# Two MLP halves apart: the up half in pairs with seven products for eight, activations through DRAM, the down half in blocks of three pairs

## The reference, cut to what matters

```python
def sq_relu_mlp(u, w1, w2):
    return jnp.square(jax.nn.relu(u @ w1)) @ w2      # w1: 1024 x 4096, w2: 4096 x 1024

h = post_norm_residual(h, y, g1, ln_g[i, 0], ln_b[i, 0])
h = post_norm_residual(h, sq_relu_mlp(modulate(h, sh2, sc2), mlp_w1[i], mlp_w2[i]), g2, ln_g[i, 1], ln_b[i, 1])
```

## Time and profile before

| what | us |
|---|---|
| median of 3 runs (lowest, highest) | 3314.88 (3314.34, 3315.09) |
| profiled execution, its span from first to last instruction | 3312.7 |
| PE busy in it | 3142.2 (95%) |
| DVE, ACT, POOL busy | 2118.3, 1329.6, 960.4 |
| mean DMA rate | 71 GB/s |

### The profile page before, as it was taken

How to read it: one execution, slowest core, us unless ns; L and a number is a source line. 1 busy time by engine, 2 the same in 40 slices (tenths; PEclk the granted TensorE clock), 3 DMA queues, 4 the chain that set the end, 5 groups by cost and what they waited for, 6 DMA issues and landing times.

```text
span 3312.7 us, 36526 instructions
## 1 busy us (share of the span) xinstructions
PE 3142.2 (95%) x14623; PEld 2589.1 (78%) x14623; DVE 2118.3 (64%) x2816; ACT 1329.6 (40%) x1877; POOL 960.4 (29%) x425
## 2 busy tenths in 40 slices
PE   7999888889999999978899999998999899999997
PEld 3888777778888888767788888887887788888886
DVE  4725477676777777585766565567697655555554
ACT  4311588454333333442633333335227443333332
POOL 0001466244444443310443333313000022222220
PEclk9999999999999999989999999999999999999999
DMA  7435211212233322111011111111111111111121
GB/s 231 145 115 178 88 45 49 89 44 72 101 102 102 102 98 81 45 41 51 26 57 52 51 51 51 51 58 52 32 52 58 58 45 51 51 51 51 51 64 51
DMA packets 190482, 235.72 MB, mean 71 GB/s; under 512 B 9671, under 2 KB 149562, under 8 KB 190314
## 3 DMA queue, kind: packets, MB, share of 16 engines
q1 hardware_dynamic: 173338, 172.90, 16.8%
q10 hardware_dynamic: 8352, 30.41, 2.6%
q0 software_dynamic: 8624, 30.09, 2.4%
HBM read 217.64 MB, written 15.73 MB: 70 GB/s over the span
## 4 chain that ended last, share of the span: by engine, by line
PE 74%; DVE 13%; ACT 8%; issue 3%; DMA 1%; POOL 0%; DVEq 0%; SPq 0%; ACTq 0%; POOLq 0%
PE psum L609 24%; PE psum L610 24%; PE psum L611 24%; DVE page_r L620 2%; DVE small L1413 2%; DVE small L742 1%; DVE PT_lo L620 1%; ACT temp L923 1%; ACT page_r L615 1%; ACT prob L1379 1%; DVE U_lo L620 1%; ACT U_hi L615 1%; DMA page<-in_ada_w_dram 1%; DVE H L1525 1%; PE psum L788 1%
## 5 line engine op out<-in xcount | busy, mean ns | idle before, releaser
L609 PE MATMUL psum<-U_hi,page_r 128*128 128x512 f32 x2108 | 832.4, 395 | 23.9 <-DVE page_r L620 11.1
L610 PE MATMUL psum<-U_lo,page_r 128*128 128x512 f32 x2108 | 826.2, 392 | 0.0
L611 PE MATMUL psum<-U_hi,page_r 128*128 128x512 f32 x2108 | 826.0, 392 | 0.0
L620 DVE TENSOR_TENSOR page_r<-page,page_r 128x1024 fp32r<-128x1024 f32 (+2 forms) x239 | 344.4, 1447 | 357.8 <-ACT page_r L615 350.6
L615 ACT CAST page_r<-page 128x1024 fp32r<-128x1024 f32 (+2 forms) x323 | 337.4, 1047 | 397.6 <-DVE page L640 95.2
L609 PEld LDWEIGHTS psum<-U_hi,page_r 128*128 128x128 f32 x2108 | 399.3, 189 | 117.3 <-DVE page_r L620 16.2
L611 PEld LDWEIGHTS psum<-U_hi,page_r 128*128 128x128 f32 x2108 | 399.0, 189 | 84.2
L610 PEld LDWEIGHTS psum<-U_lo,page_r 128*128 128x128 f32 x2108 | 399.4, 189 | 81.1
L609 PE MATMUL psum<-page_r,act_page_r 128*128 128x512 f32 x1176 | 457.5, 389 | 0.0
L610 PE MATMUL psum<-page_r,act_page_r 128*128 128x512 f32 x1176 | 457.5, 389 | 0.0
L2243 ACT ACTIVATE temp<-psum 128x512 f32<-128x512 f32 x192 | 114.6, 597 | 849.9 <-PE psum L611 805.6
(11 more groups left out here) (343 smaller groups left out, 4594.7 us busy)
## 6 DMA issues: line engine op xcount, KB each, us to landing
page<-in_mlp_w_dram SPq DMA_DIRECT2D x128, 512.0 KB, 4.1
page<-in_ada_w_dram SPq DMA_DIRECT2D x48, 512.0 KB, 5.0
page<-in_w_in_dram SPq DMA_DIRECT2D x38, 512.0 KB, 4.1
page<-in_w_up_dram SPq DMA_DIRECT2D x32, 512.0 KB, 4.1
page<-in_w_down_dram SPq DMA_DIRECT2D x32, 512.0 KB, 4.1
ada_land<-in_ada_w_dram ACTq DMA_DIRECT2D x24, 512.0 KB, 4.4
sum_page<-in_ada_w_dram ACTq DMA_DIRECT2D x12, 512.0 KB, 5.5
act_page<-in_ada_w_dram ACTq DMA_DIRECT2D x12, 512.0 KB, 8.6
```

The lines of the kernel that those rows point to most:

```text
L609: pe.matmul(out, l_hi, r_hi, start=start, stop=False, skip_group_check=read_between)
L610: pe.matmul(out, l_hi, r_lo, start=False, stop=False, skip_group_check=read_between)
L611: return pe.matmul(out, l_lo, r_hi, start=False, stop=stop, skip_group_check=read_between)
L620: return dve.tensor_tensor(lo, src, hi.bitcast(F32), ALU.subtract).then_inc(*k.lo.inc(*key))
```

## The change

Each MLP is now two phases.

Up phase (`pe_up_phase`): the 32 feature groups are 16 pairs, and a pair is again a 2 x 2 matrix (feature group by width half on one side, width half by token half on the other), made by the same seven products of 12 matmuls. The operands on the token side (U and its sums T1, T2, T4) are made once per MLP, on ACT, DVE and POOL, the sums of weights for every pair (`pool_up_sums`: e, f, c, g). Results come out of three banks A, B, C by copies of ACT and sums of DVE, named 11, 12, 21, 22 (token half first). After the square, POOL makes the four sums that the down half needs (`pool_act_folds`) for 14 of the pairs, and SP stores all to DRAM. The first three pairs do their products 1 and 2 before the second half of the tokens is transposed.

Down phase (`pe_products`, 5 blocks of 2, 3, 3, 3, 3 pairs): activations come back from DRAM by SP, split on ACT and DVE; weights by quarter, gated and summed by POOL, low parts of products 1, 2, 6, 7 on DVE and 5, 4, 3 on POOL. The last two pairs are done directly by `pe_down_tile`, 8 tiles in a row. In mlp0, H lies in DRAM during the up phase (`d_h`), and its place takes the ada pieces, four in each of the pairs 3 to 14, loaded by SP.

```diff
-BLOCKS = D_FF // (P * FB)
+PAIRS = D_FF // (2 * P)
+START = 3
+SIZES = (2, 3, 3, 3, 3)
+LAST = len(SIZES)
+RAW_PAIRS = PAIRS - sum(SIZES)
+FOLDED = PAIRS - RAW_PAIRS
...
+UP_ORDER = [(n, p) for n in range(START) for p in ("1", "2")] + [(n, p) for p in REST for n in range(2)] + \
+    [(2, p) for p in REST] + [(n, p) for n in range(START, PAIRS) for p in PRODUCTS]
...
+def up_weight(n, p):
+    if n < START:
+        return {"6": "a", "7": "c", "5": "e", "4": "d", "3": "b"}[p]
+    return {"1": "a", "2": "b", "6": "f", "7": "c", "5": "e", "4": "d", "3": "g"}[p]
...
+    def product(n, p):
+        key = (name, n, p)
+        if n < START and p in ("1", "2"):
+            on.wait_ge(*k.lo.at("w", k.unit(name, n).s))
+        else:
+            on.wait_ge(*k.lo.at("up", *key))
+        if p == "1":
+            held[n, "A"] = k.banks.take(on, ("up", name, n, "A"), (k.relu_done, (name, n, "21")), slot=n % 3)
+        elif p == "2":
+            held[n, "B"] = k.banks.take(on, ("up", name, n, "B"), (k.summed, (name, n, "11")), slot=3 + next(bank) % 5)
+        elif p == "7":
+            held[n, "C"] = k.banks.take(on, ("up", name, n, "C"), (k.summed, (name, n, "12")), slot=3 + next(bank) % 5)
+        elif p == "6":
+            on.wait_ge(*k.copied.at(name, n, "1"))
+        elif p == "5":
+            on.wait_ge(*k.copied.at(name, n, "6"))
+        elif p == "4":
+            on.wait_ge(*k.copied.at(name, n, "7"))
+        else:
+            on.wait_ge(*k.summed.at(name, n, "22"))
+        b = held[n, {"2": "B", "7": "C", "4": "C"}.get(p, "A")]
+        w_hi, w_lo = up_parts(k, name, n, p)
+        u_hi, u_lo = up_operand(k, p, 0), up_operand(k, p, 1)
+        for j in range(4):
+            if n < START:
+                if p in ("1", "2"):
+                    on.wait_ge(*k.lo.at("u", before.name, 0, j + (4 if p == "2" else 0)))
+                else:
+                    on.wait_ge(*k.lo.at("t", name, p, j))
+            s = slice(j * P, (j + 1) * P)
+            m = three_passes(pe, k.psum[:, b, :], w_hi[:, s], w_lo[:, s], u_hi[:, j, :], u_lo[:, j, :],
+                             p in ("1", "2", "7") and j == 0, j == 3, read_between=True)
+        m.then_inc(*k.up_done.inc(name, n, p))
...
+        product(n, p)
+        if p == PRODUCTS[-1] and name == "mlp0" and n in ADA_SUM_BEHIND:
+            part = ADA_SUM_BEHIND.index(n)
+            pe_ada_sum(k, pe, on, 1, part, ada_acc(k, part), slot=3 + next(bank) % 5)
...
+def sp_ada(k, sp, on, u):
+    if u.n >= ADA_RING:
+        on.wait_ge(*k.ada_x_ok.at(*k.ada_late[u.n - ADA_RING].ada))
+    else:
+        on.wait_ge(*k.h_dma[u.n].at("park"))
+        on.wait_ge(*BOUNDARY[0].hat(k, u.n))
+    sp.dma_start(u.raw, u.pieces[0][1]).then_inc(*k.ada_in[u.n % ADA_RING].inc(u.n))
...
+    for n in range(START, PAIRS):
+        folds(n - 1)
+        ada(n + 1, 0)
+        raw(n + 2, 0)
+        if n == PAIRS - 1:
+            weights(0, "11")
+            acts(0, "1")
+            weights(0, "21")
+            acts(0, "2")
+            weights(0, "12")
+            weights(0, "22")
+        square("11", n)
+        square("22", n)
+        ada(n + 1, 1)
+        raw(n + 2, 1)
+        square("12", n)
+    acts(0, "6")
...
+        on.wait_ge(*k.ada_summed.at(1, 5))
+        on.wait_ge(*k.ada_summed.at(1, 4))
+        on.wait_ge(*k.ada_x_ok.at(1, 5, KT - 1))
+        for t in range(TT):
+            on.wait_ge(*k.h_dma[t].at("park"))
+            on.wait_ge(*before.hat(k, t))
+            sp.dma_start(k.H[:, t, :], k.d_h[t]).then_inc(*k.h_dma[t].inc("back"))
+    folds(PAIRS - 1)
...
+    def step(what, x, y, op):
+        pool.tensor_tensor(at(what), at(x), at(y), op).then_inc(*k.up_folded.inc(name, n, what))
+        on.wait_ge(*k.up_folded.now())
+    for e in range(2):
+        if n >= START:
+            on.wait_ge(*k.raw_in[up_raw_page(n, e)].at(name, n, e))
+        elif e:
+            on.wait_ge(*k.raw_in[up_raw_page(n, e)].at(name, n, e))
         else:
...
+            u = k.unit(name, n)
+            on.wait_ge(*k.raw_in[u.page].at(u.n))
+            on.wait_ge(*k.lo.at("w", u.s))
+    on.wait_ge(*k.down_done.at(before.down, TT - 1, 1))
+    if n == 1:
+        on.wait_ge(*k.up_done.at(name, 2, "2"))
+    elif n >= 2:
+        on.wait_ge(*k.up_done.at(name, n - 2, "5"))
+    step("e", "c", "d", ALU.add)
+    if n < START:
+        step("c", "a", "c", ALU.subtract)
+        step("a", "e", "a", ALU.subtract)
+        step("b", "b", "a", ALU.subtract)
+        return
+    on.wait_ge(*(k.up_done.at(name, 0, "3") if n == START else k.up_done.at(name, n - 1, "6")))
+    step("f", "e", "a", ALU.subtract)
+    step("c", "a", "c", ALU.subtract)
+    if n < START + 2:
+        on.wait_ge(*k.up_done.at(name, 2, "6" if n == START else "3"))
+    else:
+        on.wait_ge(*k.up_done.at(name, n - 2, "3"))
+    step("g", "b", "f", ALU.subtract)
...
+    for which in ("11", "12", "22", "21"):
+        on.wait_ge(*k.squared.at(name, n, which))
+    if n:
+        on.wait_ge(*k.store5.at(name, n - 1, "fold 5"))
+        on.wait_ge(*k.store3.at(name, n - 1, "fold 3"))
+    step("5", s1, a21, a22, ALU.add)
+    step("7", a21, a11, a21, ALU.subtract)
+    on.wait_ge(*k.store11[n % 3].at(name, n, "11"))
+    step("6", a11, s1, a11, ALU.subtract)
+    step("3", s4, a12, a11, ALU.subtract)
...
+    act_up_start(k, act, on, name, before)
+    for n in range(START, PAIRS):
+        more = n + 1 < PAIRS
+        hi(n, "7")
+        copy(n, "1")
+        hi(n, "5")
+        square(n, "11")
+        hi(n, "4")
+        copy(n, "6")
+        hi(n, "3")
+        copy(n, "7")
+        if more:
+            hi(n + 1, "1")
+            hi(n + 1, "2")
+        square(n, "22")
+        if more:
+            hi(n + 1, "6")
         else:
...
+            parts(0, "1")
+        square(n, "12")
+        if not more:
+            parts(0, "2")
+        square(n, "21")
+    squares_stored(k, on, name)
...
+    dve_up_start(k, dve, on, name, before)
+    for n in range(START, PAIRS):
+        more = n + 1 < PAIRS
+        lo(n, "7")
+        ada(n, 0)
+        lo(n, "5")
+        if name == "mlp0" and n - 1 in ADA_SUM_BEHIND:
+            dve_mod(k, dve, on, 1, ADA_SUM_BEHIND.index(n - 1))
+        total(n, "11")
+        lo(n, "4")
+        ada(n, 1)
+        lo(n, "3")
+        if more:
+            lo(n + 1, "1")
+        ada(n, 2)
+        total(n, "22")
+        if more:
+            lo(n + 1, "2")
+        else:
+            dve_down_weight(k, dve, on, name, 0, "1")
+            dve_down_act(k, dve, on, name, 0, "1")
+        total(n, "12")
+        ada(n, 3)
+        if more:
+            lo(n + 1, "6")
+    squares_stored(k, on, name)
+    for g, (b, p) in enumerate(SEQUENCE):
+        stage = (name, b)
+        if b:
+            ready = lambda tt: on.wait_ge(*k.h_added.at((name, b - 1), "3", TPC - 1))
+        elif name == "mlp0":
+            ready = lambda tt: on.wait_ge(*k.h_dma[tt].at("back"))
+        else:
+            ready = lambda tt: on.wait_ge(*before.hat(k, tt))
+        for t in range(TPC):
+            if t == 0 and g + 1 < len(SEQUENCE):
+                dve_down_act(k, dve, on, name, *SEQUENCE[g + 1])
+            dve_quarter_tile(k, dve, on, stage, p, t, 1.0 if b else alpha, ready)
+            if t == 0 and g + 1 < len(SEQUENCE):
+                dve_down_weight(k, dve, on, name, *SEQUENCE[g + 1])
+        if (b, p) == (0, "1") and name == "mlp0":
+            dve_mod(k, dve, on, 1, 5)
+        if (b, p) in LAST_GATE_AT:
+            dve_last_gate(k, dve, on, name, LAST_GATE_AT[b, p])
...
+def pool_up_start(k, pool, on, name, b):
+    raw = lambda p, j: up_raw(k, p)[:, j, :]
+    for n in range(2):
+        pool_up_sums(k, pool, on, name, n, b)
+    for p, src, ready in (("4", "6", "6"), ("7", "3", "5")):
+        for j in range(4):
+            on.wait_ge(*k.t_vector.at(name, ready, j))
+            if p == "4":
+                x, y = raw("4", j), raw("6", j)
+            else:
+                x, y = raw("3", j), raw("7", j)
+            pool.tensor_tensor(raw(p, j), x, y, ALU.subtract).then_inc(*k.t_pool.inc(name, p, j))
+    pool_up_sums(k, pool, on, name, 2, b)
+    pool_act_folds(k, pool, on, name, 0)
+    pool_up_sums(k, pool, on, name, 3, b)
+    pool_act_folds(k, pool, on, name, 1)
...
+def pool_gate(k, pool, on, name, b):
+    if not GATE[name]:
+        return
+    on.wait_ge(*k.gate_ok.at(*GATE[name]))
+    for i, quarter in enumerate(("11", "21", "12", "22")):
+        v, c = down_raw(k, b, quarter), int(quarter[1]) - 1
+        on.wait_ge(*k.down_in[b % 2][i].at(name, b))
+        gate = k.row_gate[:, c * CH:(c + 1) * CH].unsqueeze(1).to_broadcast([P, SIZES[b], CH])
+        pool.tensor_tensor(v, v, gate, ALU.mult).then_inc(*k.pool_gated.inc("gate", name, b, quarter))
+def pool_down(k, pool, on, name, b):
+    stage = (name, b)
+    b11, b12, b21, b22, n = (down_raw(k, b, q) for q in ("11", "12", "21", "22", "N"))
+    for quarter in ("11", "21", "12", "22"):
```

(11 more changed lines are left out.)

1066 lines of the change are left out of this document (695 added, 371 removed).

## The result

| | before | after |
|---|---|---|
| median of the runs (lowest, highest), us | 3314.99 (3314.34, 3318.72) | 3438.55 (3437.18, 3441.53) |
| span of the profiled execution, us | 3312.7 | 3435.4 |

The changed kernel is slower: ratio 1.0366, 95% interval 1.0351 to 1.0381. The forecast was 3364 us, 1.5% slower, and a range up to 3430. The direction was right, the size was not: 49 us of span were forecast and 123 came.

The account below looks back on a forecast made before the run. TensorE's matmul count bounded the old kernel; chains over DVE and POOL would hold up the new. Span 3312.7 - 130.6 + 43.4 + 24 + 28 + 46 + 42.5 + 8 - 12 = 3362.0, median 3364 us, range 3255 to 3430.

Parts of the forecast that it names:

- The gain: Up and down halves: 192 matmuls fewer per MLP, 576 x 0.2267 = 130.6 us saved.
- Pairs in step: Up half, steady: no loss in mlp1 and mlp2; mlp0's period 22.07 us against 19.04, 28 us after column sums.
- rival C: Slack in mlp1's and mlp2's pairs goes, gating holds 8 blocks 4 us more each: 3423 us, chance 0.12.
- Start: Start of each MLP: a wait after the first 72 matmuls and later collisions, 67 us in all.
- The first hole: After each MLP's first 72 matmuls PE waits while DVE and POOL take turns; losses 43.4 us in all.
- X: End of an MLP's first 72 matmuls; PE was forecast to go on, in effect, at X+23.1.
- product 3 of pair 2: Start of each MLP: stands on DVE behind a low part of pair 3 that waits for POOL, 4.3 us.
- Handover: From up to down half: waits for the last square's store, H and queued activations, 46 us for three MLPs.
- Down half, steady: Blocks: product 2 waits for low weights, 12.5 us in mlp2, 15 in each gated MLP, 42.5 in all.
- Ends: MLP boundaries have less cover without two up tiles: 3 us in mlp0, 5 in mlp1, 8 in all.
- B: Side engines overlap better than turn by turn and PE stays the bound: 3239 us, faster; chance 0.23.
- D: Each stall is smaller since a late PE lets others catch up, 0.7 of 191.5: 3306 us; chance 0.15.

Follow-up runs that it names:

- e7: Changed kernel with the ada accumulations of mlp0's pairs cut to 128 of 1024 columns: 3426.5 us, 1.0320.
- e1: Changed kernel with pair 1's square 21 made by ACT behind pair 2's copies and high parts at each MLP's start: 3429.4 us, 1.0329.
- e4: Changed kernel with ACT and DVE waiting for the last squares' stores only before block 1's parts: 3440.2 us, 1.0368.
- e8: Changed kernel with last stores waited for before block 1, part of H returned earlier, product 7's activations loaded ahead of block 1's weights: 3423.9 us, 1.0310.
- e13: Changed kernel with POOL's weight sum for product 7 made behind that for product 4 in each block: 3433.7 us, 1.0344.
- e6: Changed kernel with POOL's gates and weight sums for products 5, 7 and 4 cut to 64 of 512 columns in the blocks: 3388.0 us, 1.0203.
- e5: Changed kernel without POOL's gate multiplications in the five blocks of mlp0 and mlp1: 3415.4 us, 1.0285.
- e2: Changed kernel with DVE's second four direct-pair low parts made behind product 4, not 5, in the last block: 3415.3 us, 1.0290.
- e14: Kernel of all edits together (3355.6 us), plus POOL's sum for product 7 made behind that for product 4: 3342.8 us, 1.0073.

## Why the prediction was right in direction and wrong in size

- **The gain.** 576 matmuls at the unchanged pitch; the two spans agree with the ladder within 1 us. Right.
- **Pairs in step.** mlp1 and mlp2 lose nothing on 0.6 us of forecast slack, so rival C's first half is out. mlp0's period was 20.8 us on average, not 22.1; e7 shows the cause was the one named. Right, 15 us too large.
- **Start, 67 forecast, 86 measured.** The first hole was right in kind and a little large: the wait before T's first product is up to 13.5 us, and in effect PE went on at X+20.5 to X+21, for X+23.1. That is 33 us net where 43 were forecast. What comes behind it, forecast at 24, took the rest, some 50. The failing part is the 4.3 us given to "product 3 of pair 2", where PE waits for under 0.3 us: the real second hole is before that pair's product 5, a store's round trip into the single buffer of square 21, 6.7 us and 2.4 of slow clock, three times. e1 took 12 to 17 us out.
- **Handover, 46 and 58.** The step named the right store and the right queue, but put H's return at 20 us from the last product to product 2, where 24.9 passed with the first product in it, and charged the slow clock once. e4 and e8 show that SP's order decides in mlp0 and mlp2.
- **Down half, steady, 42.5 and 91.** This is the step that failed, by its size. The chain it worked out exists (e13, e6), but its wait before product 2 came to 24 us for the 37.5 of three times 12.5 (its own 10.8 and 8.16 give 2.6 us a block, not 2.9, and in mlp0's and mlp1's last block there was no such wait). The waits before products 6 and 7, and small ones before 3, for which it had only the 5 us of the gates, were 30; e5 puts the gates' share in these blocks at 11. Missing altogether were 15 us of waits before product 3 of the last block (e2), for which the prediction has no term, and 20 us of slow clock: I charged that to three large holes and not to the 11 small ones in blocks 1 to 4, though the earlier trace rows had it behind a wait of 1.4 us. That the waits it did have a term for came to 57 us (the 24 and 30, and 3 in crumbs), near 42.5, is in part luck.
- **Ends, 8 and 15.** mlp1's direct part lost 9 us more than before, for 5 forecast. For mlp0's end I had 3: its direct part lost 4 us less than before, but the wait of Fourier's first product behind it grew from 9.82 to 18.18 us.
- **Rivals.** B (better overlap) is excluded by DVE's rows of 4.4 to 5.0 us. D is excluded too: stalls did not shrink as PE fell back. (They add up to 191.9, not 191.5, which moves D by 0.3 us.) C came out at 3423, the nearest number, and that is mostly luck: its pairs in step lost nothing, and of the 32 us that it added for gated blocks e5 finds 11 in blocks 1 to 4, where the forecast had 5.

What is not settled: why the clock stays full behind one wait of 2.36 us and not behind another of 2.35; how much of the 92 us that the starts still lose in e14 (34, 31 and 27) is DVE's own chain rather than the clock; and which of the meetings of DVE and POOL cost PE time, beyond the one place that was followed.

## What to carry to other kernels

Look, on the path that releases TensorE, for DVE operations with two SBUF inputs beside a running POOL operation, and charge each up to a whole POOL operation. Neither the total of both engines' times nor the count of all meetings foretold which version was faster. The busy shares don't show it: DVE was at 75% to 84% where PE waited. Charge the slow clock behind the small waits of TensorE too, not behind the large ones alone. Where a change sends intermediate results through DRAM, follow the one-buffer results and the order of the issuing queue to the first reader: moving a load or a square by a few places was worth 12 to 25 us each, as much as 50 to 110 matmuls.

## What the runs showed of the hardware that was not expected

- A DVE operation of 128x1536 took 1.75 us alone and 4.4 to 5.0 beside POOL's rows, up to 2.9 times; the mean over the 105 low parts of activations, of two sizes, was 2.90.
- The granted clock behind waits of equal length differed: 1.00 and 0.72 over six us behind 2.36 and 2.35 us. At one and the same wait, before product 2 of mlp2's block 2, 0.1 us was lost behind it in the trace after and 1.7 in e4's.
- In the handover of mlp0 the queues carried 411 GB/s at a share of 1.03 over ten us in which no engine computed.
